# Layer 3 of a fused three-layer kernel: norms by tile at its entry, one norm pass and the convolution's rows ahead of the last tile of values

## The reference

```python
# S = 512, D = 1024, attention and convolution 512 features each
h = rms_norm(x, g_norm1) * (1.0 + sc1) + sh1
q, k, v, ga, gb = split(h @ w_in, 512 columns each)
attn = dilated_attention(q, k, v, slopes)          # 8 heads of 64, causal, with a bias by distance
conv = conformer_conv(ga, gb, conv_w, conv_b, conv_ln_g, conv_ln_b)
x = x + gt1 * (concatenate([attn, conv]) @ w_out)
h2 = rms_norm(x, g_norm2) * (1.0 + sc2) + sh2
x = x + gt2 * hier_moe(h2, ...)                    # 32 experts, two for each token
return rms_norm(x, g_final)

def conformer_conv(a, b, conv_w, conv_b, ln_g, ln_b):
    u = a * jax.nn.sigmoid(b)
    y = causal_depthwise_conv(u, conv_w, width=31) + conv_b
    return jax.nn.silu(layer_norm(y, ln_g, ln_b))  # over the 512 channels
```

## Time and profile before

| what | value |
|---|---|
| median of the runs | 1552.5 us (1550.15 to 1552.53) |
| the profiled execution | 1549.67 us |
| its span | 1547.9 us |
| TensorE (PE) busy | 1382.1 us, 89% |
| VectorE (DVE) busy | 689.0 us, 45% |
| ScalarE (ACT) busy | 355.5 us, 23% |
| GpSimd (POOL) busy | 111.6 us, 7% |
| chain that ended last | PE 67%, DMA 17%, DVE 10% |
| mean granted clock of TensorE | 0.963 |

### The profile page before, as it was taken

One profiled execution on the slowest core, in us unless ns is written; L12 is line 12 of the kernel. 1 busy time (PEld: TensorE's weight loads), 2 busy tenths in 40 slices (PEclk: granted clock), 3 DMA queues, 4 the chain that ended last, 5 costly groups with the idle time before them and its releaser, 6 DMA issues.

```text
span 1547.9 us, 17623 instructions
## 1 busy us (share of the span) xinstructions
PE 1382.1 (89%) x6694; PEld 702.9 (45%) x6694; DVE 689.0 (45%) x1306; ACT 355.5 (23%) x778; POOL 111.6 (7%) x227
## 2 busy tenths in 40 slices
PE   4999999999999999999899989979996877868783
PEld 2444445555464444664654445456443333323331
DVE  4675524884366623322499855272221112111125
ACT  2433205562220343431400054110000000000001
POOL 3000000010100000001200000121100000000012
PEclk9999999999999999999899989989998989989897
DMA  9763136004276641003424124179999999999994
GB/s 341 271 241 112 55 109 129 1 1 163 90 254 215 203 163 55 1 1 109 145 100 162 56 109 163 55 265 395 418 417 417 422 420 421 419 419 424 424 400 174
DMA packets 85133, 338.08 MB, mean 218 GB/s; under 512 B 10343, under 2 KB 16280, under 8 KB 72376
## 3 DMA queue, kind: packets, MB, share of 16 engines
q1 hardware_dynamic: 70752, 307.24, 51.0%
q0 software_dynamic: 5664, 13.70, 3.2%
q10 hardware_dynamic: 8632, 15.99, 2.8%
HBM read 323.34 MB, written 17.24 MB: 220 GB/s over the span
## 4 chain that ended last, share of the span: by engine, by line
PE 67%; DMA 17%; DVE 10%; issue 3%; ACT 2%; POOL 1%; DVEq 0%; SPq 0%; ACTq 0%; POOLq 0%
PE score_banks L712 14%; DMA slots<-in_w_exp_up 13%; PE bank L720 13%; PE score_banks L1191 8%; PE score_banks L720 5%; PE bank L1218 4%; PE bank L928 3%; PE bank L696 3%; PE score_banks L1205 2%; PE bank L883 2%; PE bank L1030 2%; PE score_banks L1021 2%; DVE bufD L1982 2%; PE score_banks L940 1%; PE bank L944 1%
## 5 line engine op out<-in xcount | busy, mean ns | idle before, releaser
L712 PE MATMUL score_banks<-slots 128*128 128x512 f32 (+1 forms) x584 | 245.9, 579 | 6.1 <-ACTq L1350 3.5
L720 PE MATMUL bank<-slots 128*128 128x512 f32 x480 | 209.4, 593 | 2.2 <-PE bank L720 1.1
L1191 PE MATMUL score_banks<-slots,norm_row 128*64 128x512 f32 (+1 forms) x672 | 150.8, 625 | 42.8 <-DMA slots<-in_w_exp_up 42.8
L712 PEld LDWEIGHTS score_banks<-slots 128*128 128x128 f32 x584 | 112.4, 194 | 132.8 <-issue 129.4
L2473 DVE TENSOR_TENSOR mix<-probsT,score_banks 128x256 f32<-128x256 f32 (+1 forms) x39 | 14.4, 369 | 286.0 <-ACT probsT L1641 285.8
L720 PEld LDWEIGHTS bank<-slots 128*128 128x128 f32 x480 | 89.9, 190 | 113.0 <-issue 111.9
L1218 PE MATMUL bank<-slots,mix 128*64 128x512 f32 (+1 forms) x864 | 116.9, 486 | 11.5 <-issue 9.9
L1641 ACT ACTIVATE probsT<-score_banks 128x256 f32<-128x256 f32 (+1 forms) x39 | 13.4, 343 | 439.8 <-PE score_banks L1191 382.3
L1191 PEld LDWEIGHTS score_banks<-slots,norm_row 128*64 128x64 f32 (+1 forms) x672 | 52.8, 146 | 135.3 <-issue 134.9
L720 PE MATMUL score_banks<-slots 128*128 128x512 f32 (+1 forms) x256 | 95.2, 527 | 0.3 <-PE score_banks L720 0.3
L2359 DVE SCALAR_TENSOR_TENSOR bufD<-slots,col,bufD 128x512 f32<-128x512 f32 x120 | 80.5, 750 | 0.4
(11 more groups left out here) (358 smaller groups left out, 1713.3 us busy)
## 6 DMA issues: line engine op xcount, KB each, us to landing
slots<-in_w_exp_down SPq DMA_DIRECT2D x32, 2048.0 KB, 36.7
slots<-in_w_exp_gate SPq DMA_DIRECT2D x32, 2048.0 KB, 29.3
slots<-in_w_exp_up SPq DMA_DIRECT2D x32, 2048.0 KB, 34.7
slots<-in_w_in SPq DMA_DIRECT2D x16, 2048.0 KB, 8.7
slots<-in_w_mod SPq DMA_DIRECT2D x24, 1024.0 KB, 5.1
slots<-in_ada_w SPq DMA_DIRECT2D x18, 1024.0 KB, 6.3
slots<-in_w_out SPq DMA_DIRECT2D x6, 2048.0 KB, 7.8
slots<-in_ada_w SPq DMA_DIRECT2D x3, 2048.0 KB, 20.3
```

What stands on the lines that cost most here:

```text
L712: last = mm(bank[:, cols], w[:, k, lo:lo + P], src[:, k, cols], start=(k == 0), stop=(k == kts - 1))
L720: last = mm(bank[:, 0:cols], src[:, k, t * P:(t + 1) * P], rhs(k), start=(k == 0), stop=(k == kts - 1))
L1191: last = mm(out, rows[:, k, :], e_gu[it.p][:, :, k, c * pc.ff:(c + 1) * pc.ff], start=(k == 0), stop=(k == KT - 1))
```

## The change

It has four parts.

1. **Entry of layer 3.** VectorE finishes the tiles one after the other: the final norm of tile 0 stands before the residual of tile 1, and each tile is scaled soon after its final norm. `tile_rstds` and the squares of ScalarE follow in that order. The projection's product can now call something in its middle (`midway`, after four of its eight blocks): TensorE transposes tile 0 in the middle of tile 2 of the last unit, and tile 1 in the middle of tile 3. ScalarE squares tile 1 for the second time between the two halves of tile 0.
2. **The convolution's norms.** Square and sum are one instruction, the four tiles follow each other, and the first maxima come after the third tile instead of the second. The rows of tile 2 are transposed in the middle of value tile 1, those of tile 3 behind it.
3. **The normed rows.** They are transposed and go through the silu before value tile 3, not in step 4 of attention. ScalarE makes the exponentials of two steps ahead.
4. **The buffer.** The silu's results go into the upper half of `bufD` (`conv_normed`), where the convolution's sums were, instead of `hT`; `project_out` takes its blocks 4 to 7 from there (`upper_half`).

```diff
@@ -41,7 +41,6 @@
...
 MAIN = sum(ROWS_OF)
-LN_AT = 4
 OUT_AT = 6
@@ -228,6 +227,7 @@
...
         C_tok, D_tok = tok(bufC), tok(bufD)
+        conv_normed = feat(bufD, CH, 2048)
         o_raw = tok(ring[3])
@@ -713,18 +713,21 @@
...
-            def tokens(rhs, cols, kts, src, t, banks, filled):
+            def tokens(rhs, cols, kts, src, t, banks, filled, midway=lambda: None, upper_half=None):
...
                 for k in range(kts):
-                    last = mm(bank[:, 0:cols], src[:, k, t * P:(t + 1) * P], rhs(k), start=(k == 0), stop=(k == kts - 1))
+                    if k == kts // 2:
+                        midway()
+                    features_k = src[:, k, :] if upper_half is None or k < kts // 2 else upper_half[:, k - kts // 2, :]
+                    last = mm(bank[:, 0:cols], features_k[:, t * P:(t + 1) * P], rhs(k), start=(k == 0), stop=(k == kts - 1))
                 last.then_inc(filled, 1)
...
-            def project_out(kind, src, layer, last_out, norm, early, before=lambda t: None):
+            def project_out(kind, src, layer, last_out, norm, early, before=lambda t: None, midway={}, upper_half=None):
@@ -738,7 +741,8 @@
...
                                 norm(e)
-                        tokens(lambda k: w[:, k, :], W, KT, src, t, dve_banks, dve_filled)
+                        tokens(lambda k: w[:, k, :], W, KT, src, t, dve_banks, dve_filled, midway.get((u, t), lambda: None),
+                               upper_half)
                     close_unit(dve_filled, dve_banks)
@@ -777,7 +781,7 @@
...
-            def attention_pairs(rows_ready, base, scores_of, width, output_of, out, between=None, begun=False):
+            def attention_pairs(rows_ready, base, scores_of, width, output_of, out, begun=False):
@@ -803,8 +807,6 @@
...
                     flip(i)
-                    if between is not None and i == LN_AT:
-                        between()
                     if out is not None and i >= 4 and i % 4 == PAIRS_OUT_AT:
@@ -1033,7 +1035,8 @@
...
             attention_pairs(exp_ready, 32, scores1, lambda t: T, output1, out1)
-            project_out("wout1", hT, 1, lambda: out1(TT - 1), lambda t: norm_tile(2, t), {4: (0, 1)})
+            project_out("wout1", hT, 1, lambda: out1(TT - 1), None, {},
+                        midway={(1, 2): lambda: norm_tile(2, 0), (1, 3): lambda: norm_tile(2, 1)})
@@ -1069,22 +1072,25 @@
...
-            w = open_unit("win2")
-            for t in range(TT):
-                tokens(lambda k: w[:, k, :], W, KT, hT, t, tr_banks, tr_filled)
-                if t in (0, 2):
-                    conv_rows(t, t + 1)
-                elif t == 1:
-                    pe.wait_ge(qk_ready, 16 + 8)
-                    for pair in range(2):
-                        scores2([act_banks.claim(pe) for _ in range(2)], 0, pair)
-            close_unit(tr_filled, tr_banks)
-
             def norm_rows():
...
                     transposes(tr_banks, tr_filled, [lnorm[:, t, j * P:(j + 1) * P] for t in range(TT)])
+
+            w = open_unit("win2")
+            for t in range(TT):
+                tokens(lambda k: w[:, k, :], W, KT, hT, t, tr_banks, tr_filled, lambda: conv_rows(2) if t == 1 else None)
+                if t == 0:
+                    conv_rows(0, 1)
+                elif t == 1:
+                    conv_rows(3)
+                    pe.wait_ge(qk_ready, 16 + 8)
+                    for pair in range(2):
+                        scores2([act_banks.claim(pe) for _ in range(2)], 0, pair)
+                elif t == 2:
+                    norm_rows()
+            close_unit(tr_filled, tr_banks)
@@ -1098,7 +1104,7 @@
...
-            attention_pairs(scaled_ready, 0, scores2, lambda t: P * (t + 1), output2, None, norm_rows, begun=True)
+            attention_pairs(scaled_ready, 0, scores2, lambda t: P * (t + 1), output2, None, begun=True)
             pe.wait_ge(convT_ready, 1)
@@ -1107,7 +1113,8 @@
...
-            project_out("wout2", hT, 2, lambda: None, raw_tile, {2: (0,), 3: (1,), 4: (2, 3)})
+            project_out("wout2", hT, 2, lambda: None, raw_tile, {2: (0,), 3: (1,), 4: (2, 3)},
+                        upper_half=conv_normed)
@@ -1337,10 +1344,12 @@
...
-            def norm_tile(n, t):
+            def norm_tile(n, t, midway=lambda: None):
...
                 for k in range(0, KT, 4):
+                    if k > 0:
+                        midway()
                     bank = tr_banks.take(act)
@@ -1349,7 +1358,7 @@
...
-            def attention_pairs(base, width, scale, out, between=None, v_tile=None):
+            def attention_pairs(base, width, scale, out, beforehand=None):
                 n_steps = TT * HEADS // 2
@@ -1369,18 +1378,13 @@
...
-                if v_tile is not None:
-                    for t in range(TT - 1):
-                        v_tile(t)
-                exps(0)
-                if v_tile is not None:
-                    v_tile(TT - 1)
+                begun = 1 if beforehand is None else beforehand(exps)
+                if beforehand is None:
+                    exps(0)
                 for i in range(n_steps):
-                    if i + 1 < n_steps:
+                    if begun <= i + 1 < n_steps:
                         exps(i + 1)
                     copy_T(i)
-                    if between is not None and i == LN_AT:
-                        between()
                     if out is not None and i >= 4 and i % 4 == PAIRS_OUT_AT:
@@ -1559,13 +1563,12 @@
...
             square(0, 5, 0)
-            square(1, 6, 1)
-            square(0, 7, 4)
-            square(1, 8, 5)
+            square(0, 6, 4)
+            square(1, 7, 1)
+            norm_tile(2, 0, lambda: square(1, 8, 5))
             square(2, 9, 2)
-            norm_tile(2, 0)
+            norm_tile(2, 1)
             square(2, 10, 6)
-            norm_tile(2, 1)
             square(3, 11, 3)
@@ -1598,12 +1601,22 @@
...
                     bank = tr_banks.take(act)
-                    fn(hT[:, 4 + j, :], bank[:, :], ACT.Silu, bias=col2[:, R2["ln_b"] + j:R2["ln_b"] + j + 1],
+                    fn(conv_normed[:, j, :], bank[:, :], ACT.Silu, bias=col2[:, R2["ln_b"] + j:R2["ln_b"] + j + 1],
                        scale=col2[:, R2["ln_g"] + j:R2["ln_g"] + j + 1]).then_inc(tr_freed, 1)
...
-            attention_pairs(48, lambda t: P * (t + 1), -1.0, None, normed_rows, v_tile)
+            def values_and_rows(exps):
+                v_tile(0)
+                v_tile(1)
+                exps(0)
+                exps(1)
+                v_tile(2)
+                normed_rows()
+                v_tile(3)
+                return 2
+
+            attention_pairs(48, lambda t: P * (t + 1), -1.0, None, values_and_rows)
@@ -1718,7 +1731,7 @@
...
             norm_rstd(1, 8, 1)
-            tile_rstds(0, 1, 4, 5, 2, 6, 3, 7)
+            tile_rstds(0, 4, 1, 5, 2, 6, 3, 7)
             norm_rstd(W, 4, 1)
@@ -2326,12 +2339,12 @@
...
             residual_tile(0)
-            residual_tile(1)
             dve.wait_ge(norm_row_in, 16)
             final_norm_tile(0)
+            residual_tile(1)
+            scale_tile(0, 4)
             final_norm_tile(1)
             residual_tile(2)
-            scale_tile(0, 4)
             scale_tile(1, 5)
@@ -2412,9 +2425,8 @@
...
                 dve.wait_ge(dve_freed, dve_banks.n)
-                chain(v.tensor_tensor(mix[:, 0, :], lnorm[:, t, :], lnorm[:, t, :], ALU.mult))
-                chain(v.tensor_reduce(ss[:, t:t + 1], mix[:, 0, :], AX.X, ALU.add))
-                if t == 1:
+                chain(v.tensor_tensor_reduce(mix[:, 0, :], lnorm[:, t, :], lnorm[:, t, :], 1.0, 0.0, ALU.mult, ALU.add, ss[:, t:t + 1]))
+                if t == 2:
                     step_maxima(maxima2, 0)
```

## The result

The changed kernel takes 1543.88 us (median of 4 runs, 1542.28 to 1544.69), the kernel before 1552.51 beside it (4 runs, 1550.15 to 1552.91): a ratio of 0.9947, 95% interval 0.9934 to 0.9959, so 8.6 us less (6.4 to 10.2). The forecast was 1545.0 in a range of 1541 to 1550. The profiled execution took 1542.28 us with a span of 1540.6, against 1549.67 and 1547.9 before: 7.4 less, for a sum of 7.5.

What follows compares the result with a forecast made beforehand. The experts' weight transfers bound the later part, so only an earlier start of their loads gains. Terms -5.9 - 2.4 + 0.8 = -7.5 us: profiled 1549.67 to 1542.2, plus 2.8 for the median, 1545.0; range 1541 to 1550.

Steps and rivals of the forecast that it cites:

- Entry, -5.9 predicted: Entry of layer 3: VectorE's first convolution step moves from 759.86 to 753.9, -5.9 us, with bounds -7.3 and -4.
- GpSimd's hold-up: Tile 3's chain at the entry: one GpSimd step held up beside VectorE, 0 to 1.1 us, taken as 0.8.
- VectorE, not TensorE: Entry to value stage: VectorE leads, so its gain at 759.86 arrives at 879; TensorE takes the rows 1.5 us after the taps.
- Stage, -2.4: Value stage and attention's head: ninth pair 2.4 us earlier, including last value tile's +4.7; bounds -4 and +1.
- +0.8 for the clock: Sparse gap before the last value tile may lower TensorE's clock: 0 to 2.7 us lost, taken as +0.8.
- about 914: Time forecast for the ninth pair's maxima in attention's head, given as 922.2 less 5.9 and plus the clock.
- one for one: Whatever brings forward the start of the experts' weight loads, at about 950 us, comes through fully to the end.
- The two rules: Skill's claims: transposes don't count as busy for the clock (sum -5.6); table loads add a 1.38 us drain (sum -6.1).
- A: Rival: clock low through the head of attention, so only -2.8 us in all, 1549.7 us; chance 0.15.
- B: Rival: TensorE's whole gain arrives, GpSimd never held up, VectorE ready at 752.5; -10.8 us, 1541.7 us; chance 0.14.
- C: Rival: the w_mod load loop doesn't move, VectorE arrives at 879 as before, only the value stage pays; 1550.9 us; chance 0.07.
- D: Rival, slower: the last value tile's +4.7 is not paid back in attention and the entry yields little; 1556.4 us; chance 0.04.

Runs made afterwards that it cites:

- rows behind values: Changed kernel with the last value tile ahead of all four groups of transposed rows and their silus: 1542.04 us, ratio 0.9940 to the kernel before.
- two and two: Changed kernel with two groups of transposed rows and their silus ahead of the last value tile and two behind it: ratio 0.9946 to the kernel before.
- again: The changed kernel once more, without any edit: 1543.11 us, ratio 0.9943 to the kernel before.
- stage alone: Changed kernel with the entry of layer 3 as before, so only the norms and rows parts are new: 1548.64 us, ratio 0.9989 to the kernel before.
- tiles behind: Changed kernel with tiles 0 and 1 transposed behind the projection and ScalarE's squares of tiles 0 to 2 first: 1548.56 us, ratio 0.9987 to the kernel before.
- chain later: Changed kernel with two extra unused squares on ScalarE ahead of its square of tile 3, meant as 2 us delay: 1543.61 us, ratio 0.9951 to before.
- filled gaps: Changed kernel with small unread products on TensorE between the groups of transposed rows and in attention's head: ratio 0.9945 to the kernel before.
- shift product later: Changed kernel with the router's shift product between the query and key units and VectorE's add in mid-taps: ratio 0.9953 to the kernel before.
- two passes: Changed kernel with square and sum of the convolution's norms as two instructions again: ratio 0.9943 to the kernel before.
- both moves and filling: Changed kernel with shift product between query and key units, last value tile ahead of rows and silus, and unread filler products: ratio 0.9948 to before.

## Why the prediction was right

*Entry, -5.9 predicted.* Right, as the rows have it: dense work at 742.75 (predicted 742.5), first gated product at 753.61 (753.9), conv rows at 873.06 (873.5). Over the ten executions with the new order the first gated product is at 753.1 to 755.0, mean 753.8. I took 0.8 us for GpSimd's hold-up and it is 1.08 (9.57 less 8.49), of which I had seen one half, the step of 0.75 beside VectorE for 0.19; the other is that GpSimd does tile 2's second root first and starts 0.70 us behind the square, not 0.17 as at the next one (ScalarE's square ends at 750.58, GpSimd begins at 750.75).

*"VectorE, not TensorE" leads to 879.* Half wrong, and it didn't show in the number. VectorE holds TensorE at the shift; behind it TensorE is the later one wherever the clock has fallen. Both VectorE's gain at the first gated product and the gain at the conv rows are 6.2 us because the waits at the shift, 1.71 before and 2.84 after, were followed by the same loss: 64 products in 29.40 us in both traces. That is luck. With the clock kept the changed kernel's rows would have come 1.4 us earlier (an estimate: 0.11 behind the taps' end instead of 1.54), and in two of the ten executions with the new entry (rows behind values, two and two) the loss was about 1 us more. In the kernel before, the stretch behind the wait reads

```profile
816.00:818.00 2.00, 2.00 (x4) 0.50 0.91 335
```

I read the 1.5 us between the taps' end and the conv rows as a fixed step; it is TensorE's lateness. The run with the chain 1.5 us later and the one with the shift product moved show it: the step is 0.11 and 0.12 us in them.

*Stage, -2.4 and +0.8 for the clock.* Old stage 45.3 and 44.9 us, new one 44.0, 43.5, 43.8, 43.4 and 43.9 (changed, again, stage alone, tiles behind, chain later): 1.4 less on the mean, predicted 1.6. The size of the clock term (0.7 to 1.2 us by the filled gaps, in three traces) is near the 0.8 taken, its place is not the one I named: I expected it at the last value tile. That tile is slow in the first trace of the changed kernel and takes 7.13 us in the second, as with the stage alone, the tiles behind, the chain later, the shift product later and the two passes; there the head of attention pays, low for 6.8 to 10.2 us. One step was said to save 0.55 x 4 = 2.2 us, all of it on the path to the scaled rows: the single pass of squares. Taken out, it moved the transposes by 1.45 us, counted from the conv rows; the rest went into VectorE's wait for the scores, 1.42 us long in the changed kernel. Behind that ScalarE's table load covers all but 0.5, as the prediction's own times have it (transposes to 897.2, silus from 897.9), so the sum didn't suffer.

*The number "about 914"* for the ninth pair was a slip of arithmetic: 922.2 less 5.9 plus 0.8 is 917.1. It is 917.02.

*To the end, one for one.* The shift is 7.6 at attention's end, 7.2 at the first expert load, 7.3 at the end: right within 0.4 us. It was bolder than the profile bears, though. From the first expert load to the end the executions take 506.6 to 509.6 us, so one profile doesn't show 1 us there; the shift product later lost 1.5 of its 1.6 us behind that load.

*The two rules.* Seven traces have the stage's gap of 4.3 to 4.9 us in front of the last value tile, with its 16 transposes in it (the changed kernel twice, the stage alone, the tiles behind, the chain later, the two passes, the shift product later). The clock fell in one of them. The Trainium skill ("TensorE: Matmul & The Clock Gate", Part 4) says that transposes don't count as busy in the way of other matmuls. Read as in the prediction, as a sure loss, that would have lowered the clock each time, and these traces don't bear it out. The load of 1.28 us at 890.20 is followed by the silu at 891.50, and the one at 904.66 by the exponential at 905.96. The Trainium skill ("ScalarE: Activation LUTs", "What ACT_TABLE_LOAD costs") adds a drain of 1.38 us to each; these rows don't show it.

*Rivals.* A: the clock was low in the head, as it said, but at a price near 1 us, not 5. B: GpSimd was held up, so VectorE began at 753.61 and not 752.5. C: the w_mod loop moved with VectorE; its first wait for a half ends at 762.13, where it was 768.42. D: the last value tile starts 4.3 us late and the head pays it back.

## What to carry to other kernels

Before you call an engine the leader of a stretch, delay it by a known amount and see where the delay dies, and then look at the clock and the waits of the other engine in both traces: here 1.5 us vanished between two rows that I had read as rigidly tied, because TensorE had been late by as much, and because the delay had also held up TensorE at the entry and so shortened the wait that cost the clock. A delay put on one engine doesn't stay on it. A wait of TensorE can cost more than its length, for dense work behind it may run at half clock. Taking such a wait away moves it to the next place where the slower engine is met, and the loss can move with it: it did in two traces of three. And a term that reads well from its rows (0.55 us four times) needs the question what else the consumer is doing then.

## What the runs showed of the hardware

The clock behind a wait is not told by the wait's length alone. Behind waits of TensorE of 1.06 and 1.26 us at the router's shift it stayed full, behind the nine others, of 1.36 to 3.34 us, it fell. The shortest of these is the stage alone:

```profile
812.00:814.00 2.00, 1.00 (x4) 1.00 0.00 0
814.00:816.00 2.00, 2.00 (x4) 0.54 0.91 225
816.00:818.00 2.00, 2.00 (x4) 0.61 1.05 410
```

But behind one of 3.15 us at the conv rows it stayed full, and behind 3.16 and 3.31 at the same place it fell. One code can go either way: the gap of 4.3 us in front of the last value tile lowered the clock in the changed kernel's first trace and not in its second. What a fall costs is seen best at the 64 products behind the shift: 29.40 us for 27.70, so 1.7 us for 3.4 us at the lower level, and 30.4 us where the lower level lasted for 6.8 us and began in the wait.

An entry that nobody edited varies as well: with the gaps filled (an edit 150 us later) the first transposes came at 731.47, with both moves and filling at 729.55, always right behind VectorE's scaling of tile 0:

```profile
731.47 1.09 PE L696 MATMUL bank<-k_sb,slots 128*128 128x128 f32 x8 [0.35 <-DVE slots L1987]
```

```profile
729.55 1.09 PE L696 MATMUL bank<-k_sb,slots 128*128 128x128 f32 x8 [0.36 <-DVE slots L1987]
```

In the first of them tile 0's residual was already 1.92 us later (it starts at 721.65, against 719.73), so the difference comes out of layer 2, where the two programs are the same. It was not followed further. Open, too, is why 1.5 of the 1.6 us at the first expert load (shift product later) are missing at the end of that execution.
